# Compressing keys and values on 128 partitions instead of 64: token pairs on partitions, both heads in the columns

## What is computed

```python
def comp(a, w, bias):
    ch = a[:, :nch * CMP_STRIDE].reshape(B_, nch, CMP_STRIDE, N_KV, HEAD_DIM)
    ch = ch.transpose(0, 1, 3, 2, 4).reshape(B_, nch, N_KV, CMP_STRIDE * HEAD_DIM)
    wr = w.reshape(R, CMP_STRIDE * HEAD_DIM, HEAD_DIM)
    out = jnp.einsum('bckf,fd->bckd', ch[:, 0:ncmp], wr[0])
    for r in range(1, R):
        out = out + jnp.einsum('bckf,fd->bckd', ch[:, r:r + ncmp], wr[r])
    return out + bias
```

## Time and profile before

| | |
|---|---|
| runs before, median | 859.41 us (858.89 to 860.27, three runs) |
| the profiled execution, its own time | 858.78 us |
| its span in the trace | 857.0 us |
| TensorE busy | 735.6 us (86%) |
| VectorE, ScalarE, GpSimd busy | 205.8, 148.7, 183.9 us |
| HBM read and written | 239.95 and 24.92 MB |

### The profile page before, as it was taken

How to read it: one execution, slowest core, us unless ns; L and a number is a source line. 1 busy time by engine, 2 the same in 40 slices (tenths; PEclk the granted TensorE clock), 3 DMA queues, 4 the chain that set the end, 5 groups by cost and what they waited for, 6 DMA issues and landing times.

```text
span 857.0 us, 10224 instructions
## 1 busy us (share of the span) xinstructions
PE 735.6 (86%) x3645; PEld 382.9 (45%) x3645; DVE 205.8 (24%) x573; ACT 148.7 (17%) x363; POOL 183.9 (21%) x188
## 2 busy tenths in 40 slices
PE   6999999999989999689999997877777878777783
PEld 6787688887758445333333332222222222222220
DVE  2422303285768202721011010100100100100120
ACT  5223213106454311110010010000000000000000
POOL 5101000070300000013323323132132132132121
PEclk9999999999998999879999999999999999999997
DMA  9652824020610595559999999999999999999992
GB/s 303 118 152 62 277 104 106 3 75 1 252 45 1 232 424 232 197 203 409 415 407 410 412 406 406 416 414 408 413 416 406 416 413 408 415 415 408 416 414 75
DMA packets 76885, 246.52 MB, mean 288 GB/s; under 512 B 24944, under 2 KB 44303, under 8 KB 52235
## 3 DMA queue, kind: packets, MB, share of 16 engines
q1 hardware_dynamic: 63697, 230.96, 68.1%
q0 software_dynamic: 11776, 8.58, 4.5%
q10 hardware_dynamic: 1378, 6.54, 1.9%
HBM read 239.95 MB, written 24.92 MB: 309 GB/s over the span
## 4 chain that ended last, share of the span: by engine, by line
PE 45%; SPq 29%; DMA 15%; DVE 5%; issue 3%; ACT 2%; POOL 1%; ACTq 0%; POOLq 0%; DVEq 0%
PE bank L1108 42%; SPq L586 20%; DMA reg_b<-in_exp_w_gu 10%; SPq L593 9%; DMA reg_a<-in_exp_w_gu 3%; PE bank L1111 3%; DMA ffn_in<-reg_x 1%; DVE reg_a L1883 1%; DVE reg_y L2093 1%; ACT reg_y L1091 1%; DVE reg_b L1666 1%; DVE small L1843 1%; DVE reg_y L2101 1%; POOL small L691 0%; DVE reg_y L1890 0%
## 5 line engine op out<-in xcount | busy, mean ns | idle before, releaser
L1108 PE MATMUL bank<-reg_w,reg_y 128*64 128x512 f32 (+2 forms) x512 | 136.9, 572 | 15.4 <-DMA reg_w<-in_exp_w_gu 15.4
L1108 PE MATMUL bank<-reg_a,reg_y 128*64 128x512 f32 x528 | 124.3, 607 | 22.6 <-DMA reg_a<-in_exp_w_gu 16.9
L1108 PE MATMUL bank<-reg_b,reg_y 128*64 128x512 f32 x528 | 122.7, 600 | 22.3 <-DMA reg_b<-in_exp_w_gu 16.6
L2097 DVE TENSOR_TENSOR reg_y<-reg_y,bank 128x256 f32<-128x256 f32 x32 | 13.5, 421 | 418.9 <-ACT reg_y L1091 418.9
L1108 PEld LDWEIGHTS bank<-reg_w,reg_y 128*64 128x64 f32 (+2 forms) x512 | 45.4, 144 | 94.9 <-issue 54.1
L1108 PE MATMUL bank<-reg_b,reg_w 128*128 128x260 f32 x384 | 85.3, 383 | 0.0
L1108 PEld LDWEIGHTS bank<-reg_a,reg_y 128*64 128x64 f32 x528 | 34.6, 138 | 103.6 <-issue 50.6
L1108 PEld LDWEIGHTS bank<-reg_b,reg_y 128*64 128x64 f32 x528 | 34.6, 136 | 101.2 <-issue 58.0
L1108 PEld LDWEIGHTS bank<-reg_b,reg_w 128*128 128x128 f32 x384 | 72.7, 190 | 12.0 <-issue 1.1
L1111 PE MATMUL bank<-small,reg_y 128*128 128x128 f32 (+3 forms) x206 | 42.8, 317 | 24.5 <-DVE reg_y L2097 15.0
L1108 PE MATMUL bank<-reg_w,reg_b 128*128 128x256 f32 (+2 forms) x320 | 60.5, 382 | 1.1 <-DVE reg_b L1580 1.1
(11 more groups left out here) (355 smaller groups left out, 649.7 us busy)
## 6 DMA issues: line engine op xcount, KB each, us to landing
reg_a<-in_exp_w_gu SPq DMA_DIRECT2D x44, 1024.0 KB, 27.8
reg_b<-in_exp_w_gu SPq DMA_DIRECT2D x44, 1024.0 KB, 27.6
reg_w<-in_exp_w_gu SPq DMA_DIRECT2D x40, 1024.0 KB, 27.9
reg_a<-in_exp_w_down SPq DMA_DIRECT2D x22, 1024.0 KB, 28.1
reg_b<-in_exp_w_down SPq DMA_DIRECT2D x22, 1024.0 KB, 28.0
reg_h<-in_exp_w_down SPq DMA_DIRECT2D x20, 1024.0 KB, 28.1
reg_w<-in_w_in SPq DMA_DIRECT2D x9, 1024.0 KB, 11.0
reg_w<-in_w_out SPq DMA_DIRECT2D x2, 2048.0 KB, 11.1
```

The lines of the kernel that those rows point to most:

```text
L1108: return eng.matmul(out, lhsT, rhs, start=start, stop=stop, skip_group_check=True)
L2097: tt(hid[b], silu[b], bank[2 + b][:, 256:512], ALU.mult).then_inc(S["hid_made"], 1)
```

## The change

Neighbouring tokens go to different halves of the partitions. raw becomes an array with keys or values as c, the head as k, and 1280 token pairs in its columns; partitions 0 to 63 hold the 64 channels of the even token of a pair, partitions 64 to 127 those of the odd one. phi then holds, for each of 8 pairs in a chunk, the rows of the even token above those of the odd one. The compression takes 8 matmuls for keys and 8 for values instead of 32 and 32; each has 128 partitions and 320 columns, 160 chunks of each head, one in every 8 fp32 elements.

To fill raw in this layout, a sample's page is loaded with even and odd tokens side by side on 64 partitions for each page, and the four transposes of job sR become eight matmuls against the identity, each with 64 weight columns, whose results go to the lower or upper half of the PSUM partitions. Job sK keeps its transposes. For the prompt the transposes stay, and ScalarE copies each job R in four instructions of 64 partitions x 128 elements, with every second PSUM column, instead of one of 128 x 256. The compression uses two banks instead of four, ps for keys and for values, each with both heads.

```diff
-    for n in ("CK0", "CK1", "CV0", "CV1"):
-        take(n)
+    take("CK")
+    take("CV")
...
-        phi = reg_a.cut(4096, "p (c j h n) -> p c j h n", c=2, j=16, h=2)
+        phi = reg_a.cut(2048, "p (c j h n) -> p c j h n", c=2, j=8, h=2)
+        reg_a.at = 4096
...
             for c in range(2):
-                for kv in range(2):
+                for odd in range(2):
                     for half in range(2):
-                        src = a["nsa_phi"].rearrange("l c (h j d) n -> d (l c h) j n", h=2, d=HD)[:, 2 * c + half]
-                        eng.dma_start(phi[64 * kv:64 * kv + 64, c, :, kv ^ half, :], src).then_inc(S["phi_loaded"], 16)
+                        src = a["nsa_phi"][0, c].rearrange("(h j o d) n -> h o d j n", h=2, o=2, d=HD)[half, odd]
+                        eng.dma_start(phi[64 * odd:64 * odd + 64, c, :, half, :], src).then_inc(S["phi_loaded"], 16)
...
-                    eng.dma_start(page_k[k][:, g, :], rows_of_page[:, 0:384]).then_inc(smp_loaded[k], 16)
-                    eng.dma_start(vs_cache[:, b, g, :], rows_of_page[:, 384:512]).then_inc(S["vcache_loaded"], 16)
+                    pairs = rows_of_page.rearrange("(m o) f -> m o f", o=2)
+                    eng.dma_start(page_k[k][64 * g:64 * g + 64, :, :], pairs[:, :, 0:384]).then_inc(smp_loaded[k], 16)
+                    eng.dma_start(vs_cache[64 * g:64 * g + 64, b, :, :], pairs[:, :, 384:512]).then_inc(S["vcache_loaded"], 16)
...
-                    copied(copy(raw[:, :, c:c + r], ps[:, 0:256].rearrange("p (g t) -> p g t", g=2)), f"R{i}")
+                    for kv in range(2):
+                        by_pair = ps[64 * kv:64 * kv + 64, 0:256].rearrange("p (c t o) -> p c t o", c=2, o=2)
+                        for odd in range(2):
+                            ins = copy(raw[64 * odd:64 * odd + 64, :, kv, c // 2:c // 2 + 64], by_pair[:, :, :, odd])
+                    copied(ins, f"R{i}")
...
                 for c in range(2):
-                    for g in range(2):
-                        ins = turn(ps[:, 256 * c + 128 * g:256 * c + 128 * g + 128], page_k[b % PAGE_BUFS][:, g, 128 * c:128 * c + 128])
+                    for kv in range(2):
+                        at = 128 * c + 64 * kv
+                        for odd in range(2):
+                            ins = mm(ps[64 * odd:64 * odd + 64, 2 * at:2 * at + 128], page_k[b % PAGE_BUFS][:, odd, at:at + 64], ident, True, True)
...
-                for j in range(16):
-                    for kv in range(2):
-
-                        lo = 64 * kv
-                        src = raw[lo:lo + 64, comp, :].rearrange("p (n s) -> p n s", s=16)[:, :, j]
-                        ins = mm(ps2[kv][:, 0:N_CHUNK], phi[lo:lo + 64, comp, j].rearrange("p h n -> p (h n)"), src, j == 0, j == 15)
+                ps = claim(eng, name)
+                for j in range(8):
+                    src = raw[:, comp].rearrange("p k (n s) -> p k n s", s=8)[:, :, :, j]
+                    ins = mm(ps[:, 0:2 * N_CHUNK].rearrange("p (k n) -> p k n", k=2), phi[:, comp, j].rearrange("p h n -> p (h n)"), src, j == 0, j == 7)
+                filled(ins, name)
```

More of the change, by code:

```diff
@@ L238, in layer_kernel @@
         kT = reg_q.cut(2 * T, "p (r t) -> p r t", r=2)
-        raw = reg_x.t[:, :].rearrange("p (c t) -> p c t", c=2)
+        raw = reg_x.t[:, :].rearrange("p (c k t) -> p c k t", c=2, k=2)
         gain_rows = reg_y.cut(128)[0:KC]
@@ L841, in feature_qk @@
                     ps = taken(eng, f"R{i}")
-                    copied(copy(raw[:, :, c:c + r], ps[:, 0:256].rearrange("p (g t) -> p g t", g=2)), f"R{i}")
+                    for kv in range(2):
[3 more added lines that the diff above has]
+                    copied(ins, f"R{i}")
             def sample_keys(b):
                 ps = taken(eng, f"sR{b}")
-                copied(copy(raw[:, :, SEQ + PAST * b:SEQ + PAST * (b + 1)], ps[:, :].rearrange("p (c t) -> p c t", c=2)), f"sR{b}")
+                first = (SEQ + PAST * b) // 2
+                copied(copy(raw[:, :, :, first:first + 128], ps[:, :].rearrange("p (c k t) -> p c k t", c=2, k=2)), f"sR{b}")
                 if b >= 2:
@@ L876, in _ @@
             for comp, (name, out) in enumerate((("CK", kc_a), ("CV", vcT))):
+                ps = taken(eng, name)
                 for kv in range(2):
@@ L879, in _ @@
                     other = 64 - lo
-                    ps = taken(eng, f"{name}{kv}")
-                    eng.activation(out[lo:lo + 64, 0:N_CHUNK - 1], ps[other:other + 64, 1:N_CHUNK], ACT.Identity, bias=params[lo:lo + 64, P_PHI_B + comp:P_PHI_B + comp + 1]).then_inc(S["kc_copied"], 1)
+                    first = N_CHUNK * kv + 1 - kv
+                    eng.activation(out[lo:lo + 64, 0:N_CHUNK - 1], ps[other:other + 64, first:first + N_CHUNK - 1], ACT.Identity, bias=params[lo:lo + 64, P_PHI_B + comp:P_PHI_B + comp + 1]).then_inc(S["kc_copied"], 1)
             eng.wait_ge(S["kc_sum"], 1)
@@ L1232, in _ @@
             for comp, name in enumerate(("CK", "CV")):
-                ps2 = [claim(eng, f"{name}{kv}") for kv in range(2)]
-                for j in range(16):
-                    for kv in range(2):
-                        lo = 64 * kv
-                        src = raw[lo:lo + 64, comp, :].rearrange("p (n s) -> p n s", s=16)[:, :, j]
-                        ins = mm(ps2[kv][:, 0:N_CHUNK], phi[lo:lo + 64, comp, j].rearrange("p h n -> p (h n)"), src, j == 0, j == 15)
-                        if j == 15:
-                            filled(ins, f"{name}{kv}")
+                ps = claim(eng, name)
[3 more added lines that the diff above has]
+                filled(ins, name)
             def features(g, halves_of=(0, 1)):
@@ L1674, in _ @@
             for comp, (name, first, out) in enumerate((("CK", kc_a, kcT), ("CV", vcT, vcT))):
+                eng.wait_ge(S["kc_copied"], 2 * comp + 2)
+                ps = taken(eng, name)
                 for kv in range(2):
-                    lo = 64 * kv
-                    eng.wait_ge(S["kc_copied"], 2 * comp + kv + 1)
-                    ps = taken(eng, f"{name}{kv}")
-                    copied(tt(out[lo:lo + 64, 0:N_CHUNK - 1], first[lo:lo + 64, 0:N_CHUNK - 1], ps[lo:lo + 64, 0:N_CHUNK - 1], ALU.add), f"{name}{kv}")
-                    drained(eng, f"{name}{kv}")
+                    lo, at = 64 * kv, (N_CHUNK + 1) * kv
+                    ins = tt(out[lo:lo + 64, 0:N_CHUNK - 1], first[lo:lo + 64, 0:N_CHUNK - 1], ps[lo:lo + 64, at:at + N_CHUNK - 1], ALU.add)
+                copied(ins, name)
+                drained(eng, name)
                 if comp == 0:
```

## The result

The changed kernel takes 863.28 us (median of six runs, 862.46 to 864.13). The kernel before, run beside it, takes 859.98 us. The ratio is 1.004, with a 95% interval of 1.0026 to 1.0054: slower by 3.3 us (2.2 to 4.6). The profiled execution of the changed kernel took 863.58 us, 4.80 more than that of the kernel before. The forecast was 862.7 us.

The account below looks back on a forecast made before the run. TensorE was taken to bound the front and the experts' weight DMA the end, so shifts arrive whole: +3.6 samples, -0.2 compression, -0.1 lighter start give +3.3 us, 862.1, plus 0.6 for the median: 862.7 us, range 857.9 to 866.0.

Parts of the forecast that it names:

- The samples' term: Job sR, eight matmuls for four transposes: +0.6 us a sample, +3.6 us for samples 0 to 5 before RS.
- alternate halves of the output run in pairs: In sR, records alternating between lower and upper output partitions overlap in pairs, so 16 records take 0.88 us.
- The cover: TensorE's 1.41 us wait for VectorE's multiplication by RS absorbs the 1.2 us that samples 6 and 7 add.
- The compression: 16 matmuls replacing 17.53 us: 8.8 to 17.3 us, a change of -8.7 to -0.2 us, with -0.2 taken.
- Strides on both sides of 8 are slow: Reason for taking -0.2 us in the compression: slow weight loads at strides 2 and 4, slow moving operand at 16.
- The note on cachelines: Skill's rule that accesses within a 16-byte line are free; read as strides 8 and 16 costing the compression the same.
- The change of shape: One more change of matmul shape on the array in each sample, costing 0.09 us.
- The sum: Whole kernel: +3.6 - 0.2 us, less 0.1 for the lighter start of the 16 longer matmuls, gives +3.3 us.
- Stride of 8 is cheap: Rival, chance 0.20: the compression halves to 8.8 us, so the kernel gains 5.1 us and takes 854.3 us.
- Pairs do not overlap: Rival, chance 0.05: sR's 128-column matmuls run singly, 1.5 us more a sample, +10.4 us in all, 869.8 us.
- The shift is lost: Rival, chance 0.07: a wait between 250 and 386 us, or the clock by 1 to 3 us, absorbs it; 858 to 861 us.
- Edits costed at nothing: ScalarE's copies of job R (at most 1.2 us more), SP's queue, weight pieces 2.4 us later, pages, banks: all taken as 0.

Follow-up runs that it names:

- Experiment 2: Changed kernel with job sR of the samples back to four transposes instead of eight matmuls; 860.59 us, ratio 1.0002 to the kernel before.
- experiment 5: Changed kernel with sR's eight matmuls reordered, two writing the lower output half, then two the upper; one run, 861.92 us.
- the ladder: Same run as experiment 3: strides 1 to 32 tried in the changed kernel; 320-column records 269 ns apart at stride 1, 575 at 8.
- experiment 1: Changed kernel with compression matmuls reading adjacent elements instead of one in every 8 (wrong tokens); 856.18 us, ratio 0.9946 to the kernel before.
- experiment 3: Changed kernel with each compression replaced by 30 matmuls reading at strides 1 to 32; 320-column records 269 ns apart at stride 1, 563 at 4, 575 at 8.
- experiment 6: Kernel before with raw laid out place in chunk outermost, so the compression reads adjacent elements; 853.63 us (ratio 0.9921), again 850.80 us (0.9887).
- experiment 7: Changed kernel with raw laid out place of the token pair outermost, so the compression reads adjacent columns; 854.71 us (ratio 0.9949), again 855.15 us (0.9933).
- the two probes: Changed kernel with compression matmuls replaced by test reads (the ladder and a second such run); shifts of 31.3 and 27.7 us at the features, 32.8 and 30.5 at the end.

## Why the prediction was right, and where its terms were off

- **The samples' term held, its exact size by luck.** Predicted +0.6 us a sample, 1.6 us for sR and sK together; measured 1.61 against 1.02, +0.59. Six of them were to give +3.6 at RS; measured +3.64. But the samples themselves cost 3.83 (44.06 against 40.23 us from sample 0 to RS), and the profiled execution was 0.19 us ahead. Missing were two more changes of shape, for the first sample behind tile 2 and behind tile 3: before, its eight transposes followed transposes of the same shape. Its transposes took 83.68 - 82.72 = 0.96 us in the kernel before, against 1.61 now, and the four transposes ahead of it 0.44 against 0.53 (now from 84.00 to 84.53 us): +0.74 for such a sample. In the kernel before:

```profile
82.28 0.60 PE L1111 MATMUL bank<-small,reg_h 128*128 128x128 f32 x4
82.72 1.04 PE L1111 MATMUL bank<-small,reg_b 128*128 128x128 f32 x8
83.68 1.06 PE L1108 MATMUL bank<-reg_a,reg_b 128*32 128x257 f32 x4
```

  Experiment 2 takes the term away and RS is back. Part of it, that alternate halves of the output run in pairs, is true, and its condition was too narrow: the exact alternation is not needed (experiment 5).
- **The cover held.** 1.41 us of wait was to take in 1.2; 0.24 is left, and RS to compression is unchanged to 0.01 us.
- **The compression was mis-sized.** The step that failed is "a column between 0.86 ns (stride free) and 1.69 ns", with -0.2 taken. Measured: 575 ns a record, 1.80 ns a column, outside the upper bound; 18.47 us instead of 17.3, so +0.94 and not -0.2. The bound stood on the stride of 16, the only strided moving operand in my rows; the ladder shows that among 4, 5, 8, 12 and 16 it is the cheapest (538 ns), and 8 the dearest. 32 x (575 - 541) = 1.1 us is this error.
- **The reason for the bad value was half right.** "Strides on both sides of 8 are slow" leaned on the weight loads of the earlier trace rows, one in 2 or one in 4, 209 ns on average. For a moving operand 4 is slow (563) and 2 is not (281 against 269). The weight loads of one expert at stride 2 alone (379.8 to 380.3 us in the kernel before) take 208 ns, so weights and moving operands seem to differ; no run shows why. Had the stride been 2, the same argument would have failed. The argument that it is the operand's elements, and not the 64 partitions or the weights, that halve the pace of before was right: experiments 1, 3 and 6 show it directly.

```profile
L1111 PEld LDWEIGHTS bank<-small,reg_y 128*128 128x128 f32 x2 | 0.3, 208 | 0.5 <-DVE reg_y L2097 0.5
```

- **The note on cachelines.** The ladder shows the step between strides 2 and 4 and full pace with two elements in a piece of 16 bytes, at any pitch tried. The Trainium skill ("SBUF — State Buffer", "Door 1: The DMA port swizzle") asks for two hits to a line of 16 bytes for full bandwidth, and for the moving operand the runs agree (281 ns at stride 2, 563 at 4). It also says that fp32 can be strided freely up to 4; here the measurement decides: one element in 4 costs twice as much. My reading, that 8 and 16 cost the same, was off by the 7% between 575 and 538 ns, for which the note has no reason and I have none.
- **The change of shape.** I took 0.09 us for one more change of shape in each sample. The starts of single records show it: from the last pair of sR to the first transpose of sK it is 0.20 us, where pairs of one shape are 0.11 apart. These 0.09, 8 x 0.110 for the eight pairs and 0.05 for a slower first one come to 1.02, and sR takes 1.03.
- **The sum.** At the features the forecast of +3.3 was short by 1.3: +4.57, and by 1.5 without the early start. The profiled executions say +4.80 us for the whole, which fits that; the medians say +3.3 (2.2 to 4.6), since the profiled execution of before lay 1.2 us under its median of six and that of the changed kernel 0.3 above. So the median lies on the forecast by luck: one term of the sum was 1.1 us too small and another 0.2. Whether something behind the features gives back part of it on average, or the medians scatter, stays open: the interval reaches up to 4.6. (The ends of the forecast's own range, +2.3 and +4.1, come to +2.4 and +4.0 from its terms; nothing rests on that.)
- **The rivals.** *Stride of 8 is cheap* fell, though its point of decision was right: with records under 435 ns the change gains, and at 269 ns (experiment 1) it did. Its price was near: 5.1 us under the kernel before; measured, each against the kernel before on its chip, 4.4 (experiment 1) and 4.2 and 5.6 (experiment 7). *Pairs do not overlap* fell (1.03 us for 16 records, not 1.8). *The shift is lost* fell: the two probes arrive at the end whole. Its part on the clock, one to three microseconds more or less, is what the profiled executions show.
- **Edits costed at nothing** were worth nothing: the copies of R (1.11 us) and the pages (3.2 us) grew as bounded, and no wait of TensorE came from them. The weight pieces were issued at 92.22 us, not 88.78: 3.44 us late instead of 2.4, and the features did not wait. The last sample's pages start 2.46 us late, as the sum had it; most of the rest is that SP spends 0.54 us on issuing a page instead of 0.34, which I had left out.

## What to carry to other kernels

Half the partitions used is not half the pace: look in the timeline whether matmuls on different halves start together before you repack anything. Then look at the moving operand's pace per column; if it is twice that of a neighbour with adjacent elements, mend the layout where the operand is written, on an engine with time to spare, so that at least two elements of each 16 bytes are used. Moving work between transposes and matmuls in a stretch where TensorE is never idle arrives at the end whole.

## What the runs showed of the hardware that I had not expected

- fp32 moving operands: 269 ns for 320 adjacent columns, 281 at stride 2, 424 at 3, 563 at 4, 570 at 5, 575 at 8, 557 at 12, 538 at 16; 270 for two adjacent of every 16. The fall from 575 at 8 to 538 at 16 stays unexplained.
- ScalarE's copy of 128 x 512 out of PSUM takes 1.05 us with a target of stride 320 elements along its inner dimension, and 0.60 with adjacent ones.
- Matmuls whose output halves run low, low, high, high still overlap: 1.07 us against 1.03 for 16 records.
- Weight loads of 128 fp32 columns at stride 2 take 208 ns, as those at stride 4 do (210), and those of adjacent ones 147; a moving operand is hardly slower at 2.
- A page of 192 KB lands in 3.2 us on 64 partitions, two tokens in each, and in 2.5 us on 128 with one; SP takes 0.54 us to issue it instead of 0.34.
